# Encoder trunk on one core: the norm's centre from one tile, retention's values centred beforehand, low weight products last in two out tiles, and an earlier copy in the odd mixer

## The reference, cut to what matters

```python
def layer_norm(x, g, b):
    mu = jnp.mean(x, axis=-1, keepdims=True)
    var = jnp.mean(jnp.square(x - mu), axis=-1, keepdims=True)
    return (x - mu) * lax.rsqrt(var + LN_EPS) * g + b

x = layer_norm(ALPHA * x + 0.5 * swiglu_ffn(x, ...), ...)
x = layer_norm(ALPHA * x + mixer(x), ...)        # even: mLSTM and RG-LRU; odd: HGRN2 and retention
x = layer_norm(ALPHA * x + 0.5 * swiglu_ffn(x, ...), ...)
```

```python
def head_norm(x, g, n_heads, center):            # center is True for retention
    if center:
        x = x - jnp.mean(x, axis=-1, keepdims=True)   # over the 256 value features of the head
    return x * lax.rsqrt(jnp.mean(x * x, axis=-1, keepdims=True) + LN_EPS) * g

y_r = head_norm(o, norm_g, RET_HEADS, True) * silu(g)
```

## Time and profile before

| | us |
|---|---|
| Median of 3 runs | 2632.26 |
| Lowest, highest | 2629.88, 2632.73 |
| Profiled execution, its own time | 2631.72 |
| Profiled execution, span from first to last instruction | 2629.9 |
| TensorE busy | 2546.9 |
| VectorE busy | 1239.0 |
| GpSimd busy | 1056.3 |
| ScalarE busy | 889.1 |

### The profile page before, as it was taken

How to read it: one execution, slowest core, us unless ns; L and a number is a source line. 1 busy time by engine, 2 the same in 40 slices (tenths; PEclk the granted TensorE clock), 3 DMA queues, 4 the chain that set the end, 5 groups by cost and what they waited for, 6 DMA issues and landing times.

```text
span 2629.9 us, 31302 instructions
## 1 busy us (share of the span) xinstructions
PE 2546.9 (97%) x11232; PEld 2051.4 (78%) x11232; DVE 1239.0 (47%) x1347; ACT 889.1 (34%) x1080; POOL 1056.3 (40%) x447
## 2 busy tenths in 40 slices
PE   8999999998989999999999998999999999999998
PEld 6888867776766888886888886888888777788886
DVE  3333246676557333234333233566776546433324
ACT  3222136765333322213222214444444332322212
POOL 5444453222114444445444445333333233544443
PEclk9999999998999999999999998999999999999999
DMA  4333222221112233322233332222222222233332
GB/s 150 96 96 108 88 68 71 63 65 44 40 48 80 80 96 96 105 97 70 96 96 96 104 112 64 65 80 73 73 73 72 65 76 75 74 97 97 102 99 76
DMA packets 61450, 218.50 MB, mean 83 GB/s; under 512 B 10780, under 2 KB 10780, under 8 KB 61248
## 3 DMA queue, kind: packets, MB, share of 16 engines
q1 hardware_dynamic: 60944, 216.03, 26.5%
q0 software_dynamic: 432, 1.45, 0.1%
HBM read 215.36 MB, written 2.10 MB: 83 GB/s over the span
## 4 chain that ended last, share of the span: by engine, by line
PE 83%; DVE 7%; ACT 4%; issue 4%; POOL 1%; DMA 0%; SPq 0%; DVEq 0%; POOLq 0%; ACTq 0%
PE ps L448 25%; PE ps L446 25%; PE ps L447 25%; PE ps L751 2%; DVE sb_cv L1452 1%; DVE sb_th L1476 1%; DVE sb_lx L1452 1%; DVE sb_rec L1578 1%; POOL sb_wl L379 1%; POOL sb_xl L400 1%; ACT sb_th L1054 1%; PE ps L807 1%; PE ps L603 1%; PE ps L679 0%; ACT sb_la L1014 0%
## 5 line engine op out<-in xcount | busy, mean ns | idle before, releaser
L379 POOL TENSOR_TENSOR sb_wl<-sb_raw,sb_wh 128x1024 fp32r<-128x1024 f32 (+1 forms) x376 | 973.0, 2588 | 1549.3 <-ACT sb_wh L922 1549.3
L446 PE MATMUL ps<-sb_xh,sb_wh 128*128 128x512 f32 x2240 | 901.6, 403 | 33.9 <-ACT sb_xh L974 23.8
L448 PE MATMUL ps<-sb_xl,sb_wh 128*128 128x512 f32 x2240 | 885.8, 395 | 6.1 <-POOL sb_xl L400 6.0
L922 ACT ACTIVATE sb_wh<-sb_raw 128x1024 fp32r<-128x1024 f32 (+1 forms) x376 | 419.4, 1115 | 1389.5 <-PE ps L448 1386.5
L447 PE MATMUL ps<-sb_xh,sb_wl 128*128 128x512 f32 x2240 | 883.6, 394 | 0.0
L446 PEld LDWEIGHTS ps<-sb_xh,sb_wh 128*128 128x128 f32 x2240 | 428.5, 191 | 132.0 <-issue 41.9
L448 PEld LDWEIGHTS ps<-sb_xl,sb_wh 128*128 128x128 f32 x2240 | 426.4, 190 | 109.4 <-POOL sb_xl L400 21.0
L447 PEld LDWEIGHTS ps<-sb_xh,sb_wl 128*128 128x128 f32 x2240 | 428.3, 191 | 90.1 <-issue 4.1
L1318 DVE SCALAR_TENSOR_TENSOR sb_hf<-sb_sg,ps 128x512 f32<-128x512 f32 x88 | 60.5, 687 | 593.0 <-PE ps L448 593.0
L446 PE MATMUL ps<-sb_hh,sb_wh 128*128 128x512 f32 x704 | 275.5, 391 | 0.0
L448 PE MATMUL ps<-sb_hl,sb_wh 128*128 128x512 f32 x704 | 273.9, 389 | 0.0
(11 more groups left out here) (286 smaller groups left out, 2365.0 us busy)
## 6 DMA issues: line engine op xcount, KB each, us to landing
sb_raw<-w_in SPq DMA_DIRECT2D x176, 512.0 KB, 3.6
sb_raw<-w_out SPq DMA_DIRECT2D x64, 704.0 KB, 4.0
sb_raw<-w_od SPq DMA_DIRECT2D x80, 512.0 KB, 3.6
sb_raw<-w_ev SPq DMA_DIRECT2D x40, 512.0 KB, 3.6
sb_raw<-w_evo SPq DMA_DIRECT2D x8, 512.0 KB, 3.6
sb_raw<-w_odo SPq DMA_DIRECT2D x8, 512.0 KB, 3.6
sb_x<-x_in SPq DMA_DIRECT2D x8, 256.0 KB, 8.5
out<-sb_x SPq DMA_DIRECT2D x8, 256.0 KB, 2.0
```

The costliest lines, as they stand in the source:

```text
L379: pool.tensor_tensor(wl[:, sl.par, 0:n], raw[:, sl.par, 0:n], wh[:, sl.par, 0:n].bitcast(F32), ALU.subtract).then_inc(lo_done, 1)
L446: pe.matmul(out, w_h, rh(k), start=start and k == 0, stop=False)
L448: mm = pe.matmul(out, w_h, rl(k), start=False, stop=stop and k == kt - 1)
L922: act.activation(wh[:, sl.par, 0:kt * P], raw[:, sl.par, 0:kt * P], ACT.Copy).then_inc(hi_done, 1)
```

## The change

1. **Centre from tile 0.** One matmul in the rounded format, of x tile 0 alone (rounded into `xh[:, 0]` by ScalarE after VectorE's addition of tile 0) with a rounded matrix of 1/128, takes the place of the two f32 matmuls of L499. In the mixers' stages it stands after the third block of the next tile. VectorE's `residual` waits for its own second addition as well.
2. **Low products last.** In the two mixers' out phases the second pair of tiles is taken out of the loop; for these two tiles the products with the high weights come first, and those with the low weights last, with a wait for the low part only ahead of them.
3. **Splits.** In `out_splits` the splits 1 to 4 are written out, with the copy of tile 0 among them. In the odd mixer the split of out slot 1 moves into the last retention head, ahead of its root.
4. **Values centred.** VectorE takes the mean over the head's 256 value features from `vst` (`value_sum`, `value_centre`), for retention heads 0, 1, 2 at levels 4 and 5 of HGRN2 heads 2, 4 and 6, for head 3 after retention head 1. `head_mean`, `head_cen` and the centring wait go from retention; ScalarE squares the head's output straight from PSUM, VectorE adds the two tiles of squares, and the variance takes one f32 matmul. The rotation of the next queries comes after that addition.
5. **Head 0's value** is copied ahead of the sigmoid of slot 4.
6. **Constants.** `con` comes in two transfers (eight in all); the matrix of 1/128 is copied once by ScalarE into a rounded tile, which HGRN2's variance now reads too, as plain f32.

The diff, cut to its core:

```diff
@@ TensorE
+            def proj_late(bank, kt, sl, rh, rl, between=()):
+                pe.wait_ge(hi_done, sl.n + 3)
+                out = ps[:, bank, :]
+                for k in range(kt):
+                    w_h = wh[:, sl.par, k * P:k * P + P]
+                    pe.matmul(out, w_h, rh(k), start=k == 0, stop=False)
+                    pe.matmul(out, w_h, rl(k), start=False, stop=False)
+                    if k in between:
+                        between[k]()
+                pe.wait_ge(lo_done, sl.n + 3)
+                for k in range(kt):
+                    mm = pe.matmul(out, wl[:, sl.par, k * P:k * P + P], rh(k), start=False, stop=k == kt - 1)
+                mm.then_inc(w_used, 1)
...
+                def centre():
+                    pe.wait_ge(centre_in, ln + 1)
+                    pe.matmul(ps[:, 6, :], mean_r[:], xh[:, 0, :], start=True, stop=True).then_inc(mean_mm, 1)
+
                 tiles(0, first=True)
-
-                for k in range(2):
-                    pe.wait_ge(y_done, KD * ln + k + 3)
-                    mm = pe.matmul(ps[:, 6, :], cn("mean_256"), x[:, k, :], start=k == 0, stop=k == 1)
-                mm.then_inc(mean_mm, 1)
-                with pe.Fori(1, KD // 2) as i:
+                if per == 2:
+                    centre()
+                else:
+                    rh, rl = parts[0]
+                    for b in range(2):
+                        pe.wait_ge(y_done, KD * ln + b + 3)
+                        proj_late(4 + b, kt, Slot(n0, 1, 2, b), rh(False), rl, {2: centre} if b == 0 else {})
+                with pe.Fori(3 - per, KD // 2) as i:
                     tiles(i)
...
                 def squares(r):
-                    head_var(NH + r, 7, lambda z: rq[:, r % 2, z, :])
+                    pe.wait_ge(rsq_done, r + 1)
+                    pe.wait_ge(hv_done, NH + r + 1)
+                    pe.matmul(ps[:, 7, :], cn("mean_256"), rq[:, r % 2, 0, :], start=True, stop=True).then_inc(hvar_mm, 1)
...
                 of_x(2, sl(od_ret(0, 2)))
-                head_mean(NH, 6, rhv, lambda: None)
+                squares(0)
                 of_x(3, sl(od_ret(0, 3)))
-                squares(0)
...
                         of_x(1, sl(od_ret(r, 1)))
-                    head_mean(c, 6, rhv, lambda: None)
-                    if more:
-                        of_x(2, sl(od_ret(r, 2)))
                     else:
                         pe.wait_ge(part_in, KD + 2 * r)
                         early_out(r, 1)
                     squares(r)
                     if more:
+                        of_x(2, sl(od_ret(r, 2)))
                         of_x(3, sl(od_ret(r, 3)))
@@ ScalarE
+            def out_splits(n0, kt, nxt, ln, n=OUT_SLOTS, begun=1):
+
+                for j in range(begun, 5):
+                    split(kt, Slot(n0, 0, 2, j))
+                    if j == n // KD + 1:
+
+                        act.wait_ge(y_done, KD * ln + 3)
+                        act.activation(xh[:, 0, :], x[:, 0, :], ACT.Copy).then_inc(centre_in, 1)
+                with act.Fori(2, n // 2 - 1) as i:
...
                         act.activation(TA[:, d, :], ps[:, 1 + d, :], ACT.Sigmoid).then_inc(a_sig, 1)
+                    if h == 0:
+                        value(0)
                     used(sl(4 if h == 0 else od_next(h - 1, 4)))
...
                     act.wait_ge(pv_mm, c + 1)
-                    act.activation(rhv[:], ps[:, 6:8, :] if r == 0 else ps[:, 4:6, :], ACT.Copy).then_inc(hv_done, 1)
+                    o = ps[:, 6:8, :] if r == 0 else ps[:, 4:6, :]
+                    act.activation(rq[:, r % 2, :, :], o, ACT.Square).then_inc(hsq_done, 1)
+                    act.activation(rhv[:], o, ACT.Copy).then_inc(hv_done, 1)
                     if more:
                         ahead(od_ret(r, 2 if r == 0 else 1))
-                    head_square(c, rhv, rq[:, r % 2, :, :])
                     if more:
                         ahead(od_ret(r, 3 if r == 0 else 2))
+                    if not more:
+                        ahead(od_ret(r, 1))
                     head_rstd(c, rrec[:])
@@ VectorE
                 dve.wait_ge(mean_mm, 2 * ln + 1)
+                dve.wait_ge(y_done, KD * ln + 4)
...
+                def value_sum(r):
+                    dve.wait_ge(rvt_ev, HT * r + 2)
+                    step(dve.tensor_reduce(vmean[:], vst[:, HT * r:HT * r + HT, :, :].rearrange("p z b f -> p b z f"),
+                                           mybir.AxisListType.XY, ALU.add))
+                    step(dve.tensor_scalar(vmean[:], vmean[:], 1.0 / (HT * P), None, ALU.mult))
+
+                def value_centre(r):
+                    for z in range(HT):
+                        v = vst[:, HT * r + z, :, :]
+                        ins = dve.tensor_tensor(v, v, vmean[:, :, None].to_broadcast([P, NB, P]), ALU.subtract)
+                    step(ins)
...
+                        elif l == 4 and h >= 2 and h % 2 == 0:
+                            value_sum(h // 2 - 1)
+                        elif l == 5 and h >= 2 and h % 2 == 0:
+                            value_centre(h // 2 - 1)
...
+                    if not more:
+                        early_out(r, 0)
+                    sq = rq[:, r % 2, :, :]
+                    dve.wait_ge(hsq_done, c + 1)
+                    dve.tensor_tensor(sq[:, 0, :], sq[:, 0, :], sq[:, 1, :], ALU.add).then_inc(rsq_done, 1)
                     if more:
                         rope(r + 1, 0, rq, r_q, od_ret(r, 1))
-                    else:
-                        early_out(r, 0)
-                    head_cen(c, 6, rhv)
+                    dve.wait_ge(hv_done, c + 1)
...
                     early_out(r, 1)
+                    if r == 1:
+                        value_sum(NH - 1)
+                        value_centre(NH - 1)
```

More of the change, by code:

```diff
@@ L52 @@
 CON = {}
-for _name, _n in (("ident", P), ("mean_d", P), ("mean_256", P), ("mean_128", P), ("ones", P),
-                  ("tri", 2 * L), ("bd", 32)):
+for _name, _n in (("ident", P), ("mean_d", P), ("mean_256", P), ("ones", P), ("tri", 2 * L), ("bd", 32),
+                  ("mean_128", P)):
     CON[_name] = sum(n for _, n in CON.values()), _n
@@ L88, in build @@
     wl = sb("wl", [P, 2, KH * P], F32R)
-    con = sb("con", [P, NC])
+    con = sb("con", [P, NC - P])
+    mean_r = sb("mean_r", [P, P], F32R)
     vec = sb("vec", [P, NV])
@@ L372, in _ @@
             pool.sem_inc(lo_done, 2)
-            for t, name in ((con, "con"), (vec, "vec"), (mask_f, "pmask"), (w4, "w4"), (wg, "wg"), (gb, "gb"), (sel, "sel")):
+            pool.dma_start(con[:], a["con"][:, 0:NC - P]).then_inc(const_in, 16)
+            pool.dma_start(mean_f[:], a["con"][:, NC - P:NC]).then_inc(const_in, 16)
+            for t, name in ((vec, "vec"), (mask_f, "pmask"), (w4, "w4"), (wg, "wg"), (gb, "gb"), (sel, "sel")):
                 pool.dma_start(t[:], a[name]).then_inc(const_in, 16)
@@ L707, in variance @@
                     pe.wait_ge(a_sq, h + 1)
-                    pe.matmul(ps[:, 3 if h < HG - 1 else 6, :], cn("mean_128"), hsq[:], start=True,
+                    pe.matmul(ps[:, 3 if h < HG - 1 else 6, :], mean_r[:].bitcast(F32), hsq[:], start=True,
                               stop=True).then_inc(a_var, 1)
@@ L1224, in odd @@
                 front(0)
-                value(0)
                 for h in range(HG):
@@ L1259, in _ @@
             split(KD, Slot(0, 0, 2, 1))
-            act.wait_ge(const_in, 16 * 7)
+            act.wait_ge(const_in, 16 * 8)
+            act.activation(mean_r[:], mean_f[:], ACT.Copy).then_inc(mean_r_in, 1)
+            act.wait_ge(mean_r_in, 1)
             lam = vc("lam", 0, 2 * KD)
@@ L1272, in _ @@
                 if kind == "ffn":
-                    ffn(fi, n0, more)
+                    ffn(fi, n0, more, st)
                 elif kind == "even":
                     even(n0)
-                    out_splits(n0 + EV_SLOTS, KD, more, KD)
+                    out_splits(n0 + EV_SLOTS, KD, more, st, KD)
                 else:
                     odd(n0)
-                    out_splits(n0 + OD_SLOTS, KD, more, KD)
+                    out_splits(n0 + OD_SLOTS, KD, more, st, KD, 2)
                 layer_norm(st)
```

13 lines of the change are left out of this document (8 added, 5 removed).

## The result

| | before | after |
|---|---|---|
| Median of the runs of one session, us | 2632.49 (4 runs, 2629.88 to 2638.58) | 2613.92 (4 runs, 2613.40 to 2615.61) |
| Profiled execution, own time | 2631.72 | 2613.40 |
| Its span | 2629.9 | 2611.6 |

The ratio is 0.9927, with a 95% interval of 0.991 to 0.9945. The change gained 18.6 us where 25.3 were forecast, and the time lies above the range given (2602.5 to 2612).

A forecast was written before the change was run, and what follows sets the result against it. TensorE, busy 97% of the span, was taken as the bound. The terms 6.7 + 4.6 + 1.9 + 11.7 + 0.5 - 0.1 = 25.3 us took 2631.72 to 2606.4, as median 2606.9; range 2602.5 to 2612.

The forecast's parts named there:

- Norm's centre: Four FFN stages: one rounded product of 0.23 us replaces two plain f32 products costing 1.90; 6.7 us saved.
- The mixers' first out tiles: Both mixers' out phases: low products last cover GpSimd's making of low weights; 2.3 us saved twice, 4.6 us.
- rival 1: Mixers' out phases: VectorE sets their end, only some 0.7 of 2.3 us kept, twice; 2610.1 us; chance 0.13.
- rival 4: Mixers' out tiles: low weights last hides nothing, both 2.3 us lost; 2611.5 us; chance 0.04.
- The split ahead of the root in the last head: Last retention head: split of out slot 1 moved ahead of the root removes a TensorE pause; 1.9 us saved.
- Retention's values centred: Retention heads: mean products, VectorE's centring and one of two square products per head go; 11.7 us saved.
- rival 3: Retention: the chain squares, root, scaling, rotation of the next keys sets the pace; 7.8 us lost, 2614.7; chance 0.04.
- Value work: VectorE: reduction, scaling and two subtractions per value pair, 3.0 us (7.6 at upper bounds), fit idle time; cost 0.
- rival 2: Value work overflows VectorE's idle times at the upper bounds: 2 us in three heads, 2613 us; chance 0.06.
- rival 6: Mixer heads 2, 4 and 6: slow reduction makes VectorE set the pace; 51 us lost, 2658 us; chance 0.02.
- The odd mixer's first value: Odd mixer's start: ScalarE's value copy moved ahead of the gate's activation shortens TensorE's idle time; about 0.5 us saved.
- rival 5: Odd mixer's start: the lower clock behind the pause falls away, 2.0 us gained; 2604.9 us; chance 0.05.

The follow-up runs named there:

- Experiment 3: Changed kernel, with the mixers' out tiles 2 and 3 back in the old product order, low weight products no longer last, centre ahead of them: 2619.58 us.
- experiment 1: Changed kernel, with ScalarE's root in retention head 0 moved ahead of the split for slot 3: 2607.09 us, ratio 0.9904.
- experiment 2: Changed kernel, with the root moved ahead of the split for slot 2 in retention heads 1 and 2, head 0 left alone: 2613.85 us.
- experiment 6: Changed kernel, ScalarE's order kept; in head 0 VectorE rotates the next keys between variance and normalisation: 2606.60 us, ratio 0.9907.
- experiment 7: Changed kernel with head 0's root moved ahead of the split for slot 3, and the value work of every pair done twice: 2606.55 us.
- experiment 8: The changed kernel measured and profiled a second time, nothing altered: 2615.19 us, ratio 0.9937.
- experiment 5: Kernel before with only retention's values centred, plus head 0's root moved ahead of the split for slot 3: 2618.98 us, ratio 0.9951.
- experiment 4: Kernel before with only retention's values centred, nothing else of the change: 2626.99 us, ratio 0.9978.
- experiment 9: Changed kernel with head 0's root moved ahead, and in retention heads 1 and 2 the root moved behind the split for slot 3: 2619.77 us.

## Why the prediction was wrong

**Norm's centre, 6.7 us: right.** The FFN stages behind the first gained 1.81, 1.72 and 1.78 us by the table's after column (1.67 forecast), and the first 1.69 from the end of its in phase (+1.26) to its sums (-0.43). The centre product took 0.23 us, the lower of the two bounds.

**The mixers' first out tiles, 4.6: right** to 0.3 us. From the product ahead of the centre to the second behind it the kernel before took 3.01 us in the even mixer and 3.02 in the odd one, the changed kernel takes 0.87 with the centre inside: 2.1 us in each, 4.3 in all. The forecast missed the 0.33 and 0.30 us at which the first products follow. Experiment 3's 4.5 us is against its own order and not against the kernel before. That the low part, not the high part, was what TensorE waited for is shown; rivals 1 and 4 are out.

**The split ahead of the root in the last head, with that head's mean and square and the odd mixer's centre:** 1.9 + 2.9 + 0.86 + 2.3 = 8.0 us forecast, 8.03 measured (-8.54 to -16.57), and 7.99 to 8.04 in the profiles of experiments 1, 2, 6, 7 and 8, whose kernels have the same tail.

**Retention's values centred, 11.7: the term that failed.** Its parts hold: heads 1 and 2 gained 2.88 and 2.87 us in the changed kernel (forecast 2.6 to 2.7), head 0 2.6 once the root was moved, and the whole part 12.0 in experiment 5. The step that failed is the one on moved work, that after the squares there is only cover, and the number against rival 3: "four projections (21.8 us) lie between the squares and the next scores". The count is that of heads 1 and 2. In head 0 three lie there, 16.3 us. And the count starts at the wrong place: the chain starts not at the squares but when ScalarE reaches the root, which in its own list stands behind a split that waits for the first of those projections. That leaves two, 10.9 us, for a chain of 15.5. The prediction had read this queue in the last head, where the move of a split relative to the root is a term of its own, and did not read it in head 0, where the same relation had turned round. Rival 3 named the chain, gave it 7.8 us and a chance of 0.04; the chain cost 6.8 (7.1 in the second profile of the changed kernel), in one head instead of three. That its 2614.7 us lies nearer to the measured time than the forecast is luck: it took 2.6 us from each of three heads, and heads 1 and 2 lost nothing. In heads 1 and 2 it passed narrowly: the keys of head 1 were ready at 2111.75, the scores began at 2112.24, half a microsecond (experiment 1's profile).

**Value work, 3.0 us per pair at no cost: right on the cost, wrong on a part.** The reduction took 1.22 us (1.4 forecast) and the subtractions 1.29, but the scaling of four columns 1.25 to 1.73 (1.99 in the second helping of each HGRN2 head in experiment 7), forecast at 0.2 from no row. Rivals 2 and 6 are out: two helpings fitted too, but for the 0.6 us in retention. The Trainium skill, "VectorE: DVE Perf Modes", "Rules for kernel authors", expects a reduction to be the slowest operation of this engine; here its 1024 elements took as long as a product of 1024 (1.23 us).

**The odd mixer's first value, 0.5: right.** TensorE's pause went from 5.07 to 4.58 us. The stage gained 1.04 in all; the clock behind the pause came back sooner (0.84 and 0.74 in two windows of 4 us for 0.61 and 0.54), which is rival 5, by half a microsecond of its 2.0. It was no accident of one execution: the stage gained 0.99 to 1.05 in seven of the eight profiles that have this edit, and 0.15 in experiment 3's.

**Start, -0.1: not told apart from scatter.** The first FFN without its centre's 1.67 took 0.1 us more in the second profile of the changed kernel, 1.2 in the first, and 0.0 to 0.9 in the others. But the kernels of experiments 4 and 5, whose start is that of the kernel before, were 1.0 and 1.2 us later than it too.

**The sum.** With the one line moved the gain is 2631.90 - 2607.09 = 24.8 us against 25.3 forecast, and 2607.09 us stands against 2606.9. What the forecast left out was a single pause with its clock, 6.8 us. That the two medians meet to 0.2 us is partly luck: the profile of experiment 1 gained 25.9, more than forecast in retention heads 0 to 2 (8.4 us for 7.9) and at the first value (1.0 for 0.5), less in the even stage (1.9 for 2.3). Left open: the even stage, which took 1.9 to 2.2 us less in five profiles with the change, but 0.06 less in experiment 7's and 3.07 less in experiment 9's, with the same instructions in this stage; in experiments 4 and 5, whose kernels have this stage as before, it took 0.8 us more and 1.3 less than in the kernel before. The clock granted in its mLSTM part differs from execution to execution (0.74 to 0.90 from 660 to 680 us), and no run here isolated it.

**A faster version.** The changed kernel with the root (2607.09) or the keys (2606.60) moved in head 0 beats both kernels, by about 25 and 7 us; the two cures give the same.

## What to carry to other kernels

When a step is moved ahead on one engine, look up in every other engine's own list what feeds on it, and what stands ahead of that: an early input is worth nothing to an instruction queued behind a wait, and a chain's cover counts from the moment its engine is free, not from the moment its input is ready. Check each iteration by itself, the first and the last above all; here heads 1 and 2 had one projection more than head 0. And read from the profile how much reserve the consumer has before anything is taken out in front of it: 0.22 us here, against a plan to take out 2.6.

## What the runs showed of the hardware

**A pause costs more than its length.** Behind a pause of 4.79 us TensorE ran the scores at a granted clock of 0.59 (a mix of the two levels, 1.2 and 2.4 GHz) and lost 1.8 us more; in experiment 9 two such pauses of 4.79 us cost 14.4 us by the starts, not 9.6.

**Who starts first matters.** VectorE's operation on two SBUF inputs of 128x1024 took 3.29 us when GpSimd had started 0.56 us ahead of it (GpSimd's took 2.78), and 1.23 when it started 0.35 us ahead of GpSimd (GpSimd's took 3.14; the rows of the changed kernel and of experiment 1 above).

**A tiny VectorE operation can be held by GpSimd.** The scaling of 128x4 took 1.25 us where GpSimd was at work and 0.17 where it was not. The rows of experiment 9 behind its retention head 1 (GpSimd's part ended at 2114.5), against those of the changed kernel above, where the scaling ends at 1763.64 and GpSimd at 1763.61:

```profile
2116.87 1.21 DVE L1681 TENSOR_REDUCE sb_vmean<-sb_vst 128x4 f32<-128x1024 f32 x1
2118.12 0.17 DVE L1683 TENSOR_SCALAR sb_vmean<-sb_vmean 128x4 f32<-128x4 f32 x1
```

The reduction took the same 1.21 to 1.22 us beside GpSimd and without it. Both agree with the Trainium skill, "SBUF — State Buffer", "Who interferes with whom": a reduction never contends on trn2, while a scaling can enter a mode that locks the port pair shared with GpSimd. Which mode the scaling was in, no row shows. So a small operation is not a cheap one while GpSimd works.
